# A decoder step on one core: conditioning rows out of prompt attention, its weights formed by two engines

## The chip, the cores and the metric

The kernel runs on one core of a Trainium2 chip. The metric is the device time in microseconds of one execution; 0.2% of it is 6.3 us.

## The reference

Two groups go through the same two layers: a prompt of 256 tokens and 8 samples of 8 new tokens with a cache of 256 tokens each, 320 rows of 2048 floats together. Everything is fp32. Cut to what matters:

```python
def ada_modulate(c, w, b):                      # 4 times: mixer and MLP of both layers
    m = jax.nn.silu(c) @ w + b                  # w: 2048 x 6144, c: 9 rows (1 prompt, 8 samples)
    shift, scale, gate = jnp.split(m[:, None, :], 3, axis=-1)
def diff_weights(s, lam):
    p = jax.nn.softmax(s, axis=-1)
    return p[:, :, 0] - lam * p[:, :, 1]
for layer in range(2):
    h = modulated_norm(x, norm_mix, shift, scale)
    y = even_mixer(h) if layer == 0 else odd_mixer(h)   # even: 8-head attention and RG-LRU
    x = x + gate * y
    shift, scale, gate = ada_modulate(c, ada_mlp_w[layer], ada_mlp_b[layer])
    h = modulated_norm(x, norm_mlp, shift, scale)
    x = x + gate * (jnp.square(jax.nn.relu(h @ w1)) @ w2)   # w1: 2048 x 8192
```

## The kernel before

Activations lie transposed, 16 tiles of 128 features by 320 tokens. Each weight matrix streams through four slots `raw` in chunks of 512 x 256 (512 KB). ScalarE copies a chunk to `w_hi` (L604), VectorE forms `w_lo` (L982), and TensorE makes three products per tile (hi.hi, hi.lo, lo.hi) to keep fp32 accuracy. `pair` on TensorE consumes four chunks into one pair of output tiles, 24 matmuls a chunk.

The conditioning vectors come from matrices of 2048 x 6144, read once each: 16 tiles of 128 rows by 2048 columns (1.05 MB) make one part, and (a, part) names it: a = 0 to 3 for mixer and MLP of layer 0, mixer and MLP of layer 1; part = 0, 1, 2 for shift, scale, gate. `part_tile` (TensorE, L1724) multiplies one tile with the 32 columns of `cs` in four strips, adding into a PSUM bank. Once 16 tiles are in, `ada_part` (VectorE, L1041) turns the bank and adds the bias. Where the tiles are fed:

- the input projection (layer 0): (0, *) and (1,0), with rows in `narrow`;
- query and key norms: (1,1), one tile a turn through `ada_wide` (TensorE L1732, SyncE L389), six slots;
- prompt attention: (1,2), two tiles in each `p_values` (L1967);
- sample attention: (2,0), two tiles a sample;
- the MLP of layer 0: `mlp_with_parts` (TensorE L2088) with `turn_with_part` (L1767; SyncE L415, called by `feed_with_ada` L489). A block has 16 pairs of chunks for w1 and 16 for w2. Blocks 0 to 3 take (2,1), (3,0), (3,1), (3,2) through the bank `acc` during w1, a tile ahead of every second chunk, and four tiles of (2,2) each through `acc_gate` in the first four pairs of w2. `narrow` then holds one tile: SyncE waits for `narrow_used` before it loads the next one, and the raw loads are behind that wait.

Work of each engine is written out in program order, and semaphores join the engines. Around the change this order is:

- Prompt attention, VectorE: for h = 0 to 8, `p_scores(h)` (scale, mask, two maxima; L1473), then `p_weights(h-1)` (reciprocals, factor lam, first product by TENSOR_SCALAR, second by SCALAR_TENSOR_TENSOR; L1484). ScalarE: four exponentials of head h with their sums (L842), the copy of the turned weights of head h-1 (L850) and of its output (L852). TensorE: scores of h+2, then in `p_values(h)` a tile, the turn of the weights, a tile, the value product.
- Sample attention: key pages of 8 samples are loaded by GpSimd's queue (`keys`, `values`, L554 and L562), each pair as soon as the pages two samples earlier are used; a sample's queue order is keys(b+1), values(b). TensorE: scores of b, turn of keys b+1, a tile, turn of weights, a tile, values of b.
- SyncE's `ada_wide` issues tile n once tile n-6 is used.

Of the kernel before, what the change touches and what calls it, by code (L numbers as in the profile page):

```python
# [9 lines left out]
ALU = mybir.AluOpType  # L10
# [3 lines left out]
P = 128  # L14
D = 2048
# [123 lines left out]
def trunk_kernel(nc, A, O):  # L139
    with ExitStack() as ctx:  # L140
# [113 lines left out]
        acc_gate = mm[:, 2, 1, :]  # L254
# [63 lines left out]
        p_score, p_max, p_exp, p_w, p_wT, p_pt, p_o, p_out = sems("p_score p_max p_exp p_w p_wT p_pt p_o p_out")  # L318
# [39 lines left out]
        MOD_READY = [8, 15, 21, 21]  # L358
# [7 lines left out]
        def _(sp):  # L366
# [102 lines left out]
            ada_wide(1, 2)  # L469
# [19 lines left out]
            def feed_with_ada(b, a, part, after):  # L489
# [7 lines left out]
                with looped(sp, 3, KT // 2, {K: 4}) as j:  # L497
                    load_quad(inward(W2, b, j))
# [5 lines left out]
            feed_with_ada(0, 2, 1, D)  # L504
            with looped(sp, 1, BLOCKS - 1, {K: 64, KN: 20}) as b:
                feed_with_ada(b, 3, b - 1, (b + 1) * D)
            feed_with_ada(3, 3, 2, None)
# [84 lines left out]
        def _(act):  # L592
# [242 lines left out]
            for h in range(H + 1):  # L835

                if h < H:
# [66 lines left out]
            act.wait_ge(wide_used, KT * 3)  # L904
# [58 lines left out]
        def _(dve):  # L963
# [308 lines left out]
            def outward(n, squares=True, mid=None):  # L1272

                per = {K: 8, G: 2, X: 2, steps: 2}
                if squares:
                    step(v.memset(sq_sum[:, :, :], 0.0))
                    settle()
                    per |= {SQ: 2, steps: 4}
                if mid is not None:
                    split()  # L1280
                    residual(0, 0, n, squares=squares)
                    split()
                    residual(1, 2, n, squares=squares)
                    mid()
                with looped(dve, 0 if mid is None else 1, 3 if squares else 4, per) as i:
# [24 lines left out]
            def mlp(n, last, parts=False):  # L1310
# [10 lines left out]
                def block_(ahead, part=None, squares=False, gate=False):  # L1321
# [5 lines left out]
                    if part is not None:  # L1327
                        NU.up(16)
                        ada_part(*part, acc, narrow_used, NU.now)
                        NU.up(4)  # L1330
                    if ahead:
                        outward(n, squares, (lambda: ada_part(2, 2, acc_gate, narrow_used, NU.now)) if gate else None)
# [9 lines left out]

                per = {G: 8, R: 8, U: 8, X: 8, steps: 8}
                if parts:
                    NU.up(24)
                    block_(1, (2, 1))
                    with looped(dve, 1, BLOCKS - 1, {K: 64, AG: 1, AT: 1, NU: 20, **per}) as b:
                        block_(1, (3, b - 1))
                    block_(1, (3, 2), squares=True, gate=True)
# [134 lines left out]
            def p_weights(h):  # L1484
# [5 lines left out]
                for k in (5, 7):  # L1490
                    step(v.tensor_tensor(small[:, r, k:k + 1], small[:, r, k:k + 1], lam[:, 0:1], ALU.mult))
                settle()
                for qb in range(2):
# [695 lines left out]
```

## Time and profile before

| | us |
|---|---|
| median of 3 runs | 3152.55 (3146.82 to 3153.94) |
| the profiled execution | 3152.81 |
| its span in the profile | 3151.1 |
| TensorE busy (share of the span) | 3056.1 (97%) |
| VectorE busy | 1480.9 (47%) |
| ScalarE busy | 1084.4 (34%) |
| moved by DMA | 624.90 MB, mean 198 GB/s |

The times of rows are microseconds from the start of the span. PE is TensorE (PEld its weight loads), DVE VectorE, ACT ScalarE, POOL GpSimd, SP SyncE. A bracket at the end of a timeline line gives the idle time of the engine before it and what ended it. An fp32 matmul has more than one record here (x8 is one tile of four matmuls). PEclk is the granted clock of TensorE in parts of 2.4 GHz, DMA share the mean busy share of the 16 engines.

### The profile page before, as it was taken

What the parts mean: (1) busy time and instruction counts of PE and PEld (TensorE: products, weight loads), DVE (VectorE), ACT (ScalarE), POOL (GpSimd) and SP (SyncE); (2) the same over time, 40 slices, a digit from 0 to 9 for tenths busy, and PEclk for the clock granted to TensorE, in tenths of its full rate; (3) what the DMA queues carried; (4) which work ended last, traced back from release to release, by engine and by line L of the source; (5) the groups of instructions that cost most, each with busy time, mean ns of one, the idle gap of its engine ahead of it and who ended that gap; (6) DMA issues with size and microseconds to landing.
All of it is one profiled execution on the core that took longest, in us unless ns stands there. A gap on an engine that the chain in (4) does not pass through costs nothing.

```text
span 3151.1 us, 53269 instructions
## 1 busy us (share of the span) xinstructions
PE 3056.1 (97%) x21011; PEld 2809.6 (89%) x21011; DVE 1480.9 (47%) x2057; ACT 1084.4 (34%) x1309; POOL 29.6 (1%) x55
## 2 busy tenths in 40 slices
PE   8999997899999999999999899999999999999998
PEld 4888853598899899889889899999899999999998
DVE  3556555455344344344345554445544444444443
ACT  3334443334322332332333433333433332332332
POOL 0000001000000000000000000000000000000000
PEclk8999998999999999999999999999999999999999
DMA  9986789545765765765774344444344444444543
GB/s 317 338 284 225 259 346 417 206 155 194 256 199 196 258 218 182 253 235 160 261 253 147 121 149 150 142 153 150 124 148 151 143 152 147 142 152 141 152 149 107
DMA packets 451959, 624.90 MB, mean 198 GB/s; under 512 B 16960, under 2 KB 402753, under 8 KB 433028
## 3 DMA queue, kind: packets, MB, share of 16 engines
q1 hardware_dynamic: 443776, 595.65, 57.1%
q0 software_dynamic: 6112, 22.84, 1.9%
q10 hardware_dynamic: 1926, 4.24, 0.4%
q8 instruction: 119, 1.95, 0.3%
q14 instruction: 26, 0.21, 0.0%
HBM read 617.13 MB, written 5.54 MB: 198 GB/s over the span
## 4 chain that ended last, share of the span: by engine, by line
PE 92%; DMA 4%; DVE 2%; issue 1%; ACT 1%; SPq 0%; POOL 0%; POOLq 0%; DVEq 0%; ACTq 0%
PE mm L1672 86%; PE aux L1672 5%; PE mm L1825 1%; DMA wide_first<-in_ada_mix_w 1%; DMA narrow<-in_ada_mlp_w 1%; DMA kpage<-in_cache_k 1%; DVE tmp L1063 1%; DMA vpage<-in_cache_v 1%; DMA second_row<-in_ada_mlp_w 0%; DVE h_lo L1089 0%; PE aux L2043 0%; DVE tmp L1079 0%; DVE tmp L1082 0%; DVE w_lo L982 0%; PE aux L1825 0%
## 5 line engine op out<-in xcount | busy, mean ns | idle before, releaser
L982 DVE TENSOR_TENSOR w_lo<-raw,w_hi 128x1024 fp32r<-128x1024 f32 x752 | 919.6, 1225 | 1325.9 <-ACT w_hi L604 1324.3
L604 ACT ACTIVATE w_hi<-raw 128x1024 fp32r<-128x1024 f32 x752 | 794.8, 1058 | 1703.9 <-PE mm L1672 1703.9
L1672 PE MATMUL mm<-h_hi,w_hi 128*128 128x320 f32 x3712 | 1167.6, 315 | 32.3 <-DVE h_lo L1089 18.9
L1672 PE MATMUL mm<-h_hi,w_lo 128*128 128x320 f32 x3712 | 1152.8, 311 | 0.0
L1672 PE MATMUL mm<-h_lo,w_hi 128*128 128x320 f32 x3712 | 1152.6, 311 | 0.0
L1672 PEld LDWEIGHTS mm<-h_hi,w_hi 128*128 128x128 f32 x3712 | 701.9, 189 | 132.8 <-issue 104.6
L1672 PE MATMUL mm<-u_hi,w_hi 128*128 128x320 f32 x2304 | 713.7, 310 | 0.0
L1672 PE MATMUL mm<-u_hi,w_lo 128*128 128x320 f32 x2304 | 712.0, 309 | 0.0
L1672 PE MATMUL mm<-u_lo,w_hi 128*128 128x320 f32 x2304 | 711.9, 309 | 0.0
L1672 PEld LDWEIGHTS mm<-h_lo,w_hi 128*128 128x128 f32 x3712 | 702.6, 189 | 0.2 <-issue 0.2
L1672 PEld LDWEIGHTS mm<-h_hi,w_lo 128*128 128x128 f32 x3712 | 702.2, 189 | 0.0
L1672 PEld LDWEIGHTS mm<-u_hi,w_hi 128*128 128x128 f32 x2304 | 432.5, 188 | 13.4 <-issue 13.4
L1672 PEld LDWEIGHTS mm<-u_lo,w_hi 128*128 128x128 f32 x2304 | 432.5, 188 | 0.0
L1672 PEld LDWEIGHTS mm<-u_hi,w_lo 128*128 128x128 f32 x2304 | 432.5, 188 | 0.0
L1672 PE MATMUL aux<-narrow,cs 128*32 128x512 f32 x856 | 122.0, 609 | 2.2 <-DMA narrow<-in_ada_mlp_w 2.2
L1318 DVE TENSOR_TENSOR u_lo<-mtmp,u_hi 128x640 f32 x64 | 52.8, 826 | 67.0 <-ACT u_hi L746 67.0
L746 ACT ACTIVATE u_hi<-mtmp 128x640 f32 x64 | 47.3, 739 | 98.5 <-DVE mtmp L1315 98.5
L1253 DVE SCALAR_TENSOR_TENSOR xT<-mm,mod,xT 128x256 f32 (+1 forms) x160 | 69.4, 476 | 0.0
L1315 DVE TENSOR_TENSOR mtmp<-mtmp 128x640 f32<-128x640 f32 x64 | 52.5, 820 | 0.0
L1672 PE MATMUL aux<-wide_first,cs 128*32 128x512 f32 x232 | 45.1, 679 | 5.8 <-DMA wide_first<-in_ada_mix_w 4.9
L744 ACT ACTIVATE mtmp<-mm 128x640 f32<-128x640 f32 x64 | 43.9, 686 | 0.0
L707 ACT ACTIVATE tmp<-tmp,mod,amp 128x256 f32<-128x256 f32 x64 | 34.0, 590 | 23.0 <-DVE amp L1070 14.6
(280 smaller groups left out, 1071.5 us busy)
## 6 DMA issues: line engine op xcount, KB each, us to landing
raw<-in_mlp_w SPq DMA_DIRECT2D x512, 512.0 KB, 3.7
narrow<-in_ada_mlp_w SPq DMA_DIRECT2D x70, 1024.0 KB, 5.0
raw<-in_w_in_odd SPq DMA_DIRECT2D x96, 512.0 KB, 3.8
narrow<-in_ada_mix_w SPq DMA_DIRECT2D x42, 1024.0 KB, 5.1
raw<-in_w_in_even SPq DMA_DIRECT2D x80, 512.0 KB, 6.9
wide_first<-in_ada_mix_w SPq DMA_DIRECT2D x58, 512.0 KB, 9.0
wide_later<-in_ada_mlp_w SPq DMA_DIRECT2D x20, 1024.0 KB, 14.3
raw<-in_w_out_even SPq DMA_DIRECT2D x32, 512.0 KB, 3.5
```

What stands on the lines that cost most here:

```text
L604: fn(w_hi[:, slot], raw[:, slot], ACT.Copy).then_inc(hi_ready, 1)
L707: ins = fn(out, out, ACT.Identity, scale=amp[:, k, 0:1], bias=mod[:, n, k, 0:1])
L744: fn(mtmp[:, r], mm[:, r, :, 0:T], ACT.Relu).then_inc(relu_out, 1)
L746: fn(u_hi[:, bass.ds(j, 2), :], mtmp[:, r], ACT.Copy).then_inc(u_hi_ready, 1)
L982: v.tensor_tensor(w_lo[:, slot], raw[:, slot], w_hi[:, slot].bitcast(F32), ALU.subtract).then_inc(lo_ready, 1)
L1063: v.tensor_tensor(tmp4[:, first // 4 % 2, first % 4:first % 4 + count], xT[:, first:first + count, :], rstd[:, :].unsqueeze(1).broadcast_t ...
L1253: ins = v.scalar_tensor_tensor(x, mm[:, r, m, 0:SEQ], g, x, ALU.mult, ALU.add)
L1315: v.tensor_tensor(mtmp[:, r], mtmp[:, r], mtmp[:, r], ALU.mult).then_inc(u_val, 1)
L1318: v.tensor_tensor(u_lo[:, bass.ds(j, 2), :], mtmp[:, r], u_hi[:, bass.ds(j, 2), :].bitcast(F32), ALU.subtract).then_inc(u_ready, 1)
L1672: return nc.tensor.matmul(out, lhsT, rhs, start=first, stop=last)
L1825: return nc.tensor.transpose(out, in_, const[0:rows, 0:rows])
```

## The change

Prompt attention has no conditioning tiles any more. (2,0) follows (1,1) directly in the six slots and is used in sample attention as before. (1,2) moves into the first MLP block through `acc`, which moves (2,1) to block 1, (3,0) to block 2 and (3,1) to block 3; (3,2) gets a bank of its own, `acc_last`, four tiles in each block, in pairs 5 to 8 of w2 (the second call of `turn_with_part` on `u_hi`). The 80 tiles of this MLP become 96. VectorE turns (1,2) after w1 of block 0 and waits for it before the first residual; it turns (2,2) and (3,2) in the last block after four residuals instead of (2,2) after two. In prompt attention ScalarE makes the first product (a copy with a column scale), and VectorE's reciprocals of head h-1 stand ahead of the scores of head h. Where loops had a common body, block by block is now written out.

```diff
@@ SyncE
             ada_wide(1, 1, 2)
-            ada_wide(1, 2)
             ada_wide(2, 0)
...
                 turn_with_part(inward(W2, b, 1), 2, 2, b * (4 * P), inward(W2, b, 2))
-                with looped(sp, 3, KT // 2, {K: 4}) as j:
+                turn_with_part(inward(W2, b, 3), 3, 2, b * (4 * P), inward(W2, b, 4))
+                with looped(sp, 5, KT // 2, {K: 4}) as j:
                     load_quad(inward(W2, b, j))
...
-            feed_with_ada(0, 2, 1, D)
-            with looped(sp, 1, BLOCKS - 1, {K: 64, KN: 20}) as b:
-                feed_with_ada(b, 3, b - 1, (b + 1) * D)
-            feed_with_ada(3, 3, 2, None)
+            feed_with_ada(0, 1, 2, D)
+            feed_with_ada(1, 2, 1, 2 * D)
+            feed_with_ada(2, 3, 0, 3 * D)
+            feed_with_ada(3, 3, 1, None)
@@ ScalarE
             for h in range(H + 1):
+                if h >= 1:
+                    r = (h - 1) % 2
+                    act.wait_ge(p_part, h)
+                    for qb in range(2):
+                        part = p_s[:, r, 0, 0:P] if qb == 0 else p_s[:, r, 0, P:384]
+                        ins = fn(part, part, ACT.Copy, scale=small[:, r, 4 + 2 * qb:5 + 2 * qb])
+                    ins.then_inc(p_first, 1)
...
-            act.wait_ge(wide_used, KT * 3)
+            act.wait_ge(wide_used, KT * 2)
@@ VectorE
+                with looped(dve, 0, 2, per) as i:
+                    split()
+                    residual(0, i * 4, n, squares=squares)
+                    split()
+                    residual(1, i * 4 + 2, n, squares=squares)
                 if mid is not None:
-                    split()
-                    residual(0, 0, n, squares=squares)
-                    split()
-                    residual(1, 2, n, squares=squares)
                     mid()
-                with looped(dve, 0 if mid is None else 1, 3 if squares else 4, per) as i:
+                with looped(dve, 2, 3 if squares else 4, per) as i:
...
                         ada_part(*part, acc, narrow_used, NU.now)
-                        NU.up(4)
+                        NU.up(8)
+                        dve.wait_ge(mod_ready, AG.now)
...
+                def last_parts():
+                    ada_part(2, 2, acc_gate, narrow_used, NU.now - 4)
+                    ada_part(3, 2, acc_last, narrow_used, NU.now)
...
-            def p_weights(h):
+            def p_parts(h):
                 r = h % 2
                 dve.wait_ge(p_exp, h + 1)
                 step(v.reciprocal(small[:, r, 4:8], small[:, r, 4:8]))
                 settle()
-                for k in (5, 7):
-                    step(v.tensor_tensor(small[:, r, k:k + 1], small[:, r, k:k + 1], lam[:, 0:1], ALU.mult))
-                settle()
-                for qb in range(2):
-                    keys = slice(0, P) if qb == 0 else slice(P, 384)
-                    step(v.tensor_scalar(p_s[:, r, 0, keys], p_s[:, r, 0, keys], small[:, r, 4 + 2 * qb:5 + 2 * qb], None,
-                                         ALU.mult))
-                settle()
+                step(v.tensor_tensor(small[:, r, 5:6], small[:, r, 5:6], lam[:, 0:1], ALU.mult))
+                v.tensor_tensor(small[:, r, 7:8], small[:, r, 7:8], lam[:, 0:1], ALU.mult).then_inc(p_part, 1)
+
+            def p_weights(h):
+                r = h % 2
+                dve.wait_ge(p_part, h + 1)
+                settle()
+                dve.wait_ge(p_first, h + 1)
                 for qb in range(2):
...
             for h in range(H + 1):
+                if h >= 1:
+                    p_parts(h - 1)
                 if h < H:
                     p_scores(h)
...
-                if b == 0:
-                    ada_part(1, 2, acc, wide_used, 2 * KT)
@@ TensorE
             def p_values(h):
                 r = h % 2
-                ada_wide()
                 pe.wait_ge(p_w, h + 1)
...
                 ins.then_inc(p_wT, 1)
-                ada_wide()
                 pe.wait_ge(p_pt, h + 1)
...
                     turn_with_part(u_hi, u_lo, acc_gate, 4 * b, u_block(),
                                    ((relu_out, relu - 1), lambda: (relu_out, relu)))
-                    with looped(pe, 1, 4, {K: 8, G: 2}):
+                    turn_with_part(u_hi, u_lo, acc_last, 4 * b, None, (None, None))
+                    with looped(pe, 2, 4, {K: 8, G: 2}):
```

## Rows read from the trace of the kernel before

**Rows 1.** The page, part 4: shares of the chain that ended last.

```profile
...
PE 92%; DMA 4%; DVE 2%; issue 1%; ACT 1%; SPq 0%; POOL 0%; POOLq 0%; DVEq 0%; ACTq 0%
...
```

**Rows 2.** Windows: prompt attention, then sample attention (header: columns).

```profile
...
core 0: us, PE busy (x) PEld busy (x) DVE busy (x) ACT busy (x) POOL busy (x), PEclk, DMA share, GB/s
...
468.30:516.10 47.80, 39.51 (x264) 17.30 (x264) 29.85 (x83) 21.08 (x80) 3.23 (x6) 0.86 1.02 420
516.10:599.40 83.30, 68.18 (x944) 39.86 (x944) 34.12 (x116) 12.97 (x24) 13.67 (x26) 0.92 0.85 345
...
```

**Rows 3.** Chain of waits, 400 to 630: start us, us, what held it.

```profile
...
497.94 15.76 DMA narrow<-in_ada_mlp_w
...
524.46 21.18 DMA kpage<-in_cache_k
...
```

**Rows 4.** Timeline of DVE, sample attention: three of eight score evacuations (start us, us).

```profile
...
521.38 0.42 DVE L1536 TENSOR_SCALAR s_s<-mm 128x256 f32<-128x256 f32 x1 [1.50 <-PE mm L1672]
...
584.89 0.42 DVE L1536 TENSOR_SCALAR s_s<-mm 128x256 f32<-128x256 f32 x1 [7.35 <-PE mm L1672]
...
593.03 0.42 DVE L1536 TENSOR_SCALAR s_s<-mm 128x256 f32<-128x256 f32 x1 [3.27 <-PE mm L1672]
...
```

**Rows 5.** Timeline of PE in sample attention: two stalls on page transfers.

```profile
...
539.06 0.64 PE L2043 MATMUL aux<-vpage,s_pt 128*32 128x128 f32 x16 [2.21 <-DMA vpage<-in_cache_v]
...
545.68 3.68 PE L1825 MATMUL mm<-const,kpage 128*128 128x128 f32 x16 [2.40 <-DMA kpage<-in_cache_k]
...
```

**Rows 6.** Chain of waits, an MLP block of layer 0.

```profile
...
1118.06 0.99 PE aux L1672 x8
1119.06 124.62 PE mm L1672 x848
...
```

**Rows 7.** Chain of waits, layer 1: one whole MLP block.

```profile
...
2449.23 225.68 PE mm L1672 x1536
...
```

**Rows 8.** Groups of instructions in the MLP block of rows 6.

```profile
...
L982 DVE TENSOR_TENSOR w_lo<-raw,w_hi 128x1024 fp32r<-128x1024 f32 x64 | 78.4, 1226 | 139.0 <-ACT w_hi L604 139.0
...
```

**Rows 9.** Timeline of DVE in prompt attention.

```profile
...
491.25 0.96 DVE L1478 SCALAR_TENSOR_TENSOR p_s<-mm,const 128x768 f32<-128x768 f32 x1 [0.71 <-PE mm L1825]
...
493.17 0.17 DVE L1488 RECIPROCAL small<-small 128x4 f32<-128x4 f32 x1
...
493.64 0.55 DVE L1495 TENSOR_SCALAR p_s<-p_s,small 128x128 f32<-128x128 f32 x2
494.23 0.75 DVE L1500 SCALAR_TENSOR_TENSOR p_s<-p_s,small 128x128 f32<-128x128 f32 x2
495.69 0.96 DVE L1478 SCALAR_TENSOR_TENSOR p_s<-mm,const 128x768 f32<-128x768 f32 x1 [0.72 <-PE mm L1825]
...
509.24 0.18 DVE L1488 RECIPROCAL small<-small 128x4 f32<-128x4 f32 x1 [3.28 <-ACT p_s L842]
...
```

**Rows 10.** Timeline of ACT in prompt attention.

```profile
...
507.07 0.38 ACT L852 ACTIVATE pj<-aux 128x256 f32<-128x256 f32 x1 [4.43 <-PE aux L1672]
507.36 0.39 ACT L842 ACTIVATE p_s<-p_s,small 128x128 f32<-128x128 f32 x1
...
507.74 0.39 ACT L842 ACTIVATE p_s<-p_s,small 128x128 f32<-128x128 f32 x1
...
509.11 0.47 ACT L850 ACTIVATE p_t<-mm 128x384 f32<-128x384 f32 x1
...
```

**Rows 11.** Timeline of PE in prompt attention.

```profile
...
475.94 0.90 PE L1825 MATMUL mm<-const,p_s 128*128 128x128 f32 x3 [1.08 <-DVE p_s L1500]
...
483.19 0.94 PE L1672 MATMUL aux<-p_t,vtok 128*128 128x128 f32 x6
...
505.57 1.47 PE L1672 MATMUL aux<-p_t,vtok 128*128 128x128 f32 x6
...
```

**Rows 12.** One line, L707: ns min/median/max of one, over the span.

```profile
...
L707 ACT ACTIVATE tmp<-tmp,mod,amp x64: 583/587/603, 51.5 to 2227.8; 128x256 f32<-128x256 f32 x64
...
```

**Rows 13.** Window at the start of prompt attention, columns of rows 2.

```profile
...
470.00:475.00 5.00, 4.14 (x19) 1.13 (x16) 4.83 (x13) 2.66 (x13) 1.13 (x2) 0.50 1.01 421
...
```

More of the change, by code:

```diff
@@ L253, in trunk_kernel @@
         acc = aux[:, 1, :]
-        acc_gate = mm[:, 2, 1, :]
+        acc_gate, acc_last = mm[:, 2, 1, :], mm[:, 2, 0, :]
         folded = mm[:, 2, 1, 448:448 + 4 * NC]
@@ L317, in trunk_kernel @@
         tok_t, tok_ready = sems("tok_t tok_ready")
-        p_score, p_max, p_exp, p_w, p_wT, p_pt, p_o, p_out = sems("p_score p_max p_exp p_w p_wT p_pt p_o p_out")
+        p_score, p_max, p_exp, p_part, p_first, p_w, p_wT, p_pt, p_o, p_out = sems(
+            "p_score p_max p_exp p_part p_first p_w p_wT p_pt p_o p_out")
         tab_in = sems("tab_in")
@@ L357, in trunk_kernel @@
         GAIN = [ROW["norm_mix"], ROW["norm_mlp"], ROW["norm_mix"] + KT, ROW["norm_mlp"] + KT]
-        MOD_READY = [8, 15, 21, 21]
+        MOD_READY = [8, 14, 21, 21]
         H_READY = [0, 10, 16, 22]
@@ L1329, in block_ @@
                         ada_part(*part, acc, narrow_used, NU.now)
-                        NU.up(4)
+                        NU.up(8)
+                        dve.wait_ge(mod_ready, AG.now)
                     if ahead:
-                        outward(n, squares, (lambda: ada_part(2, 2, acc_gate, narrow_used, NU.now)) if gate else None)
+                        outward(n, squares, last_parts if gate else None)
                     else:
@@ L1345, in mlp @@
                     NU.up(24)
+                    block_(1, (1, 2))
                     block_(1, (2, 1))
-                    with looped(dve, 1, BLOCKS - 1, {K: 64, AG: 1, AT: 1, NU: 20, **per}) as b:
-                        block_(1, (3, b - 1))
-                    block_(1, (3, 2), squares=True, gate=True)
+                    block_(1, (3, 0))
+                    block_(1, (3, 1), squares=True, gate=True)
                 else:
@@ L1559, in _ @@
                               ).then_inc(s_pte, 1)
-            ada_part(2, 0, acc, wide_used, 3 * KT)
+            ada_part(2, 0, acc, wide_used, 2 * KT)
             dve.wait_ge(s_root, 1)
@@ L2090, in mlp_with_parts @@
                 for b in range(BLOCKS):
-                    pe.wait_ge(ada_turned, b + 4)
+                    pe.wait_ge(ada_turned, b + 3)
                     turn_with_part(h_hi, h_lo, acc, 0, h_inputs(count),
```

## The prediction

> **What bounds the kernel now.** I read the page first. Its chain of waits is TensorE for 92% of the span and DMA for 4% [rows 1], so nearly everywhere a microsecond of TensorE work is a microsecond of time, and DMA decides only in some stretch. The question is which. Windows by stage answer it: in prompt attention (468.3 to 516.1, 47.8 us) the DMA share is 1.02 at 420 GB/s, TensorE is busy 39.51 us of 47.80; in sample attention (516.1 to 599.4, 83.3 us) DMA runs at 345 GB/s on average and TensorE is busy 68.18 us [rows 2]. The chain inside this stretch, read next, goes through transfers: the last conditioning rows for 15.76 us, then a key page for 21.18 us [rows 3]. So these two stages are partly DMA-bound, and everything behind them is TensorE-bound. The change takes 16 transfers of 1.05 MB (128 rows of 2048 floats) out of the DMA-bound part and puts them, with the TensorE work that belongs to them, where TensorE is the bound. It trades one against the other, and the sum is that of both.
>
> **Sample attention.** First I look for the undisturbed pace. The eighth score evacuation comes 593.03 - 584.89 = 8.14 us after the seventh, with no DMA wait between; the first comes 521.38 - 516.1 = 5.3 us after the stage begins, and the stage ends 599.4 - 593.03 = 6.4 us after the eighth [rows 2, 4]. Undisturbed the stage is 5.3 + 7 x 8.14 + 6.4 = 68.7 us. It takes 83.3, so waits for transfers (and the slower TensorE beside them) hold 14.6 us. That is the upper bound of the gain here.
>
> How much of it goes? The stage still consumes per sample two conditioning tiles, one pair of key pages and one pair of value pages, four units of 1.05 MB in 8.14 us: 515 GB/s, against 420 served [rows 2]. It can only run at the undisturbed pace from stock and by a growing backlog. Stock: in the new order the six tile slots are refilled with rows of (2,0) as the query/key stage uses up (1,1), and nobody uses them in prompt attention, so six tiles, two key pairs and one value pair lie ready; today the queue is full when the stage begins. Left to come are 10 tiles, 6 key pairs and 7 value pairs: 23 units, 24.1 MB, 57 us at 420 GB/s, which just fits into 62 us. But the shares of the two queues decide. A value wait ended at 539.06 and the key wait behind it on GpSimd's queue at 545.68: with SyncE's queue also full, one unit of pages takes 6.6 us [rows 5], that is 0.159 of 0.420 MB/us, 38%. From 2.6 us after the start until the tiles begin (8.2 us) the pages have the engines alone, 2.5 us a unit: 2.2 units. SyncE then gets 0.26 MB/us, 4.0 us a tile, so its 10 tiles keep it busy until about 48 us; in these 40 us the pages get 6.0 units, 8.2 in all. At the undisturbed pace PE wants its ninth page unit at about 46 us. So some 0.8 units (5 us at this share) are missing there once, with landing on top; afterwards the pages have the engines alone and catch up. I take 5 us of stall left, gain 9.6. Bounds: 14.6, and 4 (the stage begins with five tiles less queued, 12 us of transfers, of which at least a third should show).
>
> The Trainium skill, DMA: Bandwidth & Descriptors, "Queues, rings and completion order", says that each DMA engine takes turns between the queues that have work, a packet each. Equal packets would give the pages half of the bandwidth, a unit in 5 us instead of the 6.6 of rows 5, and the missing 0.8 units would be there in time; the trace speaks against an even share. What the sum would be by an even share is the third rival.
>
> **The MLP.** Sixteen tiles are added in front of pairs of weight chunks: four per block on (3,2) in the second down pair, while the others keep their number. What does one cost? A stretch of 17 chunk pairs and 4 tiles takes 124.62 us [rows 6]. A block of layer 1 without tiles takes 225.68 us for 1536 matmuls, 32 chunk pairs of 48: 7.05 us each [rows 7]. So 4 tiles take 124.62 - 17 x 7.05 = 4.7 us, 1.18 us each; the 0.99 of the chain's own row for the tile [rows 6] misses the slowed first weights behind it. The cost is 16 x 1.18 = 18.8 us. All of it is on the path. Bounds: 15.8 (0.99 each) and 18.9.
>
> What else comes with it, at nothing: the 16 transfers (2.5 us each at 420 GB/s) go to `narrow`, one slot, and SyncE waits on it with the raw loads behind; it did so for 80 tiles already, in blocks where TensorE never waited, and VectorE sits idle 139 us of a 249 us block before its weight halves [rows 8], which is the cover. If it failed, each raw load that came late would cost its lateness. The turning of (1,2) and (3,2) (about 1 us of VectorE each) lies in the same cover, as does the new wait for `mod_ready` in front of the first residual, behind which stand a split and the residual; both have a chunk pair of 7 us. Loops written out or re-entered cost VectorE and SyncE sequencer time only.
>
> **Prompt attention.** Its undisturbed period today is 495.69 - 491.25 = 4.44 us a head [rows 9], in which the two tiles on TensorE and the chain scores, reductions, weights, turn just fit. The change takes the tiles away (2 us of TensorE), and the first factor from VectorE (494.23 - 493.64 = 0.59 us [rows 9]). But it also puts the reciprocal of head h-1 in front of the scores of head h, and that waits for ScalarE's exponentials. The new circle: exponentials 509.24 - 507.36 = 1.88 us from their start to the reciprocal [rows 9, 10]; reciprocal and factors 0.47; scores and maxima 493.17 - 491.25 = 1.92 [rows 9]; a handover of 0.03. That is 4.30 us. The other circle, through ScalarE: exponentials to the copy of the turned weights 509.11 - 507.36 = 1.75, that copy 0.47, PE's value product 0.94 [rows 11] with 0.10 of handovers, the output copy 0.29 to the next start, and the two new scaled copies [rows 10]. For these I have no row. Nearest are the exponentials with one column operand on the same tiles, 0.39 and, by the stretch from 507.36 to 509.11, about 0.49, less the overlap of 0.1 each: 0.69. The upper bound is twice L707, 128x256 with two column operands: 1.17 [rows 12]; the lower two plain copies, 0.5. I take 0.69, since shape and operands are nearest: 4.24 us, just under 4.30. By the Trainium skill, ScalarE: Activation LUTs, "What ACT_TABLE_LOAD costs", each column pointer adds about 93 ns; a copy with one pointer would then cost what the exponential does without its read-out, again 0.69, while L707 has two.
>
> So VectorE's relief is eaten by the new order: the period falls only from 4.44 to 4.30, and the gain is the DMA waits. In full: first scores 1 us after 468.3, maxima 1.92 later (471.2), exponentials to 473.1, factors and second scores to 475.5; six periods to 501.3 for the eighth maxima; then exponentials, value product and output of the head before, its own copies (4.24), products 0.75, turn some 0.6 (0.90 at the low clock [rows 11]), copy, value product, output copy with handovers 2.0: 7.6, so 508.9 against 516.1. Gain 7.2 with TensorE at full clock.
>
> Its clock is the doubt. With two tiles of 0.99 us [rows 6] gone, TensorE pauses 2 us more in every head. After the pauses at the beginning of this stage the granted clock was 0.50, the lower level of 1.2 GHz [rows 13]; there the turn took 0.90 and a value product 1.47 (full clock: 0.94) [rows 11]. ScalarE's circle then is 4.24 + 0.53 = 4.77. With half of the heads like that it costs 3.5 x 0.47 = 1.6, and 0.6 more in tail and at the start of the sample stage. Gain 7.2 - 2.2 = 5.0. Bounds: 7.2, and 7.2 - 7 x 0.95 = 0.5 with the low clock throughout and copies at their upper bound (period 5.25).
>
> **Sum.** 18.8 - 9.6 - 5.0 = +4.2 us. The profiled execution took 3152.8 us (span 3151.1 and 1.7 around it), the median of three runs 3152.55, so both are one level: 3157.0 us. A measurement of this kernel tells 0.2% (6.3 us) from nothing; the forecast is no measurable change, leaning to slower.
>
> **The rivals.**
> 1. Slower: the pages stay late. GpSimd's queue keeps its 6.6 us a unit and falls behind earlier than I count, so that 11 of the 14.6 us of stall stay. For it: demand is over supply all the time, and a stall also lowers TensorE's clock (the 3.68 us turn behind a wait [rows 5]). Against it: the stock at the start. Price: 18.8 - 3.6 - 4 = +11, 3164. It decides slower once more than 7 us of stall stay with the prompt gain at 5.
> 2. Slower: TensorE stays at the low clock through prompt attention and into the first samples. The prompt stage gains 1, the sample stage 8: +10, 3163. For it: rows 13. Against: the clock of prompt attention averages 0.86 [rows 2], so it came back within the stage, beside DMA waits that now go.
> 3. No change from the other side: full clock and no stall: 18.8 - 7.2 - 14.6 = -3, 3150. With an even share of the queues (a page unit in 2 x 2.5 = 5 us beside SyncE's, 8 instead of 6 in the 40 us, nothing missing at 46 us) it comes out near here: 1 us of stall and prompt gain 5, so 18.8 - 13.6 - 5 = +0.2, 3153. The even share is the rule of the skill's page named above.
> 4. Faster: rival 3's gains in full, and the moved tiles hide a part of their 1.18 us under the matmuls around them (0.75 each, 7 us less): 3143. For it: a tile uses 32 columns of TensorE. Against: [rows 6] show no such overlap.
> 5. The cover fails: SyncE's waits delay raw loads. One chunk late by 2 us per block, +8: 3165. Nothing in 80 tiles shows it.
>
> **How the numbers follow.** Chances: forecast 0.48, rival 1 0.20, rival 2 0.10, rival 3 0.13, rival 4 0.06, rival 5 0.03. Slower by over 0.2%: rivals 1, 2 and 5, less a little near the line, plus the upper edge of the forecast: 0.33. Faster: 0.07. Within: 0.60. The range runs from rival 3 to rival 1: 3149 to 3165.
>
> **What would show it.** Blocks of layer 0's MLP longer by 4.7 us each (249.0 to 253.7) show the cost; any other growth says that tiles or waits are priced wrong. Prompt attention of 40 to 47 us with DMA mostly idle in its second half; a period of 4.3, or 4.8 where the granted clock is 0.5. In sample attention a period of 8.14 for the first five or six samples, and a page wait of about 5 us once near the end; stalls from the third sample on would show rival 1. The forecast is wrong if the two stages together gain under 12 us or over 25.

## The result and the profile after

The changed kernel takes 3163.29 us (median of 9 runs, 3158.06 to 3168.18), the kernel before 3149.89 (9 runs beside it, 3146.31 to 3153.94): ratio 1.0041, 95% interval 1.0032 to 1.0050. It is slower by 13.4 us, by more than the 0.2% that a measurement tells. The forecast was 3157.0, +4.2, inside "no measurable change". The profiled executions stand only 8.1 us apart (3160.94 and 3152.81, spans 3159.3 and 3151.1); of the 5.3 us between that and the medians, 2.9 are the profiled execution before, which lay above its median, and 2.4 the changed one, which lay below.

The page of the changed kernel, shares of the chain that ended last; it answers to [rows 1]:

```profile
PE 93%; DMA 2%; DVE 2%; ACT 1%; issue 1%; SPq 0%; POOL 0%; POOLq 0%; DVEq 0%; ACTq 0%
```

DMA went from 4% to 2%: half of the time on transfers left the path. Windows of the changed kernel for prompt and sample attention (columns of [rows 2]), then its first five microseconds of scores, which answer to [rows 13]:

```profile
467.56:511.79 44.23, 25.15 (x137) 17.20 (x137) 25.47 (x67) 26.50 (x96) 3.23 (x6) 0.72 0.44 176
511.79:591.79 80.00, 67.06 (x949) 40.47 (x950) 34.49 (x116) 16.39 (x37) 13.68 (x26) 0.95 0.76 303
...
469.00:474.00 5.00, 1.18 (x11) 0.53 (x8) 3.90 (x10) 2.66 (x10) 1.14 (x2) 0.97 1.00 419
```

Prompt attention was bound by DMA (share 1.02); now DMA stands at 0.44, and TensorE's mean granted clock fell from 0.86 to 0.72. The first scores ran at full clock this time (0.97 against 0.50); the low clock came later, with 0.50 between 475 and 480. The stage gained 47.85 - 44.23 = 3.6 us. Sample attention, by DVE's score evacuations ([rows 4]), third to fifth and last of eight:

```profile
534.55 0.42 DVE L1554 TENSOR_SCALAR s_s<-mm 128x256 f32<-128x256 f32 x1 [3.27 <-PE mm L1688]
543.86 0.42 DVE L1554 TENSOR_SCALAR s_s<-mm 128x256 f32<-128x256 f32 x1 [4.45 <-PE mm L1688]
557.23 0.42 DVE L1554 TENSOR_SCALAR s_s<-mm 128x256 f32<-128x256 f32 x1 [3.42 <-PE mm L1688]
...
581.63 0.42 DVE L1554 TENSOR_SCALAR s_s<-mm 128x256 f32<-128x256 f32 x1 [3.27 <-PE mm L1688]
```

The eighth comes 581.63 - 511.79 = 69.84 us after the stage begins; before it was 76.89 (593.03 - 516.14). Two intervals are longer than 8.14: 9.31 and 13.37, 6.4 us more. They are page waits, with a slower turn of the keys behind the second (2.73 for 1.97). PE's timeline, answering to [rows 5]:

```profile
540.65 0.64 PE L2057 MATMUL aux<-vpage,s_pt 128*32 128x128 f32 x16 [1.43 <-DMA vpage<-in_cache_v]
...
547.79 2.73 PE L1841 MATMUL mm<-const,kpage 128*128 128x128 f32 x16 [4.00 <-DMA kpage<-in_cache_k]
```

In the chain (start, us, what) the first row below lies under both waits; the second ends in a wait of only 0.23 us. These two answer to [rows 3], the third, an MLP half of layer 0 with w2, to [rows 6]:

```profile
529.49 18.26 DMA kpage<-in_cache_k
...
560.30 13.32 DMA kpage<-in_cache_k
...
1113.47 129.37 PE mm L1688 x880
```

The half took 124.62 for x848 before: 4.75 us more, 32 matmuls more being the four tiles. In DVE's groups the cover of [rows 8] is intact (141.5 us idle ahead of `w_lo` in a block).

Prompt attention of one head at full clock, ACT's timeline (start us, us, ...), answering to [rows 10]; new are the scaled copies, L843:

```profile
495.24 0.47 ACT L859 ACTIVATE p_t<-mm 128x384 f32<-128x384 f32 x1
496.74 0.38 ACT L861 ACTIVATE pj<-aux 128x256 f32<-128x256 f32 x1 [1.02 <-PE aux L1688]
497.02 0.79 ACT L843 ACTIVATE p_s<-p_s,small 128x128 f32<-128x128 f32 x2
...
499.53 0.47 ACT L859 ACTIVATE p_t<-mm 128x384 f32<-128x384 f32 x1
```

and PE's for the end of one such head and for the next, which fell to the low clock ([rows 11]):

```profile
500.05 0.94 PE L1688 MATMUL aux<-p_t,vtok 128*128 128x128 f32 x6 [0.76 <-ACT p_t L859]
503.02 0.90 PE L1841 MATMUL mm<-const,p_s 128*128 128x128 f32 x3 [2.04 <-DVE p_s L1516]
504.50 1.65 PE L1688 MATMUL aux<-p_t,vtok 128*128 128x128 f32 x6 [0.58 <-ACT p_t L859]
```

The period is 499.53 - 495.24 = 4.29, as forecast. At the low clock a value product takes 1.65, and the head 5.09.

Stage by stage, from the profiles (us). A profile is one execution, a median is that of 6 to 12, and each ratio is to the kernel before as it ran beside that experiment, with medians of 3149.89 to 3151.24. ("prompt" runs from the first scores to the first turn of keys, "samples" from there to the eighth evacuation, "MLP 0" from its norm's squares to those of the next; "last MLP" is layer 1's, from its norm's squares to the turning of the output, which the change does not touch.)

| kernel | prompt | samples | MLP 0 | last MLP | median | ratio to before, 95% |
|---|---|---|---|---|---|---|
| before | 47.85 | 76.89 | 1007.66 | 924.77 | 3149.89 | |
| changed | 44.23 | 69.84 | 1026.67 | 924.06 | 3163.29 | 1.0041, 1.0032 to 1.0050 |
| split_only | 47.83 | 78.43 | 1007.71 | 923.30 | 3149.62 | 0.9999, 0.9990 to 1.0008 |
| move_only | 42.67 | 70.69 | 1026.63 | 924.72 | 3157.82 | 1.0021, 1.0012 to 1.0030 |
| no_last_part | 47.91 | 71.35 | 1007.64 | 924.58 | 3142.56 | 0.9973, 0.9963 to 0.9984 |
| idle_tiles | 43.64 | 68.36 | 1026.64 | 923.82 | 3159.97 | 1.0030, 1.0021 to 1.0040 |
| copies_first | 41.06 | 73.99 | 1026.64 | 923.66 | 3158.37 | 1.0025, 1.0015 to 1.0034 |
| early_page | 44.24 | 69.87 | 1026.67 | 924.50 | 3161.30 | 1.0036, 1.0024 to 1.0048 |
| sample_from_memory | 47.90 | 63.13 | 1026.63 | 926.19 | 3156.93 | 1.0016, 1.0007 to 1.0025 |
| half_moved | 42.74 | 75.79 | 1024.53 | 921.33 | 3155.91 | 1.0020, 1.0011 to 1.0029 |
| before_early_page | 50.36 | 72.15 | 1007.64 | 921.62 | 3149.89 | 0.9999, 0.9990 to 1.0007 |
| gap_tiles | 47.76 | 80.04 | 1006.16 | 925.17 | 3149.38 | 0.9998, 0.9989 to 1.0007 |
| copies_idle | 42.29 | 68.25 | 1027.39 | 915.10 | 3149.80 | 1.0005, 0.9995 to 1.0014 |
| short_tiles | 47.89 | 70.92 | 1026.66 | 915.11 | 3152.99 | 1.0008, 0.9997 to 1.0020 |

### The profile page after: what moved, and what is told of

Its sections match the earlier page's. It is cut to its first block, busy times and chain, and to the rows that moved or that the text cites. A ratio compares the mean times of both kernels' runs of the same rounds, so it can differ in the third digit from the quotient of the medians.

```text
span 3159.3 us, 52905 instructions
## 1 busy us (share of the span) xinstructions
PE 3056.7 (97%) x21011; PEld 2811.7 (89%) x21011; DVE 1476.3 (47%) x2041; ACT 1089.8 (34%) x1325; POOL 29.6 (1%) x55
## 3 DMA queue, kind: packets, MB, share of 16 engines
q10 hardware_dynamic: 1926, 4.24, 0.4%
## 4 chain that ended last, share of the span: by engine, by line
PE 93%; DMA 2%; DVE 2%; ACT 1%; issue 1%; SPq 0%; POOL 0%; POOLq 0%; DVEq 0%; ACTq 0%
PE mm L1688 87%; PE aux L1688 5%; PE mm L1841 1%; DMA kpage<-in_cache_k 1%; DMA wide_first<-in_ada_mix_w 1%; DMA second_row<-in_ada_mlp_w 0%; DVE tmp L1072 0%; ACT p_s L851 0%; DVE h_lo L1098 0%; PE aux L2057 0%; DVE tmp L1088 0%; DVE tmp L1091 0%; ACT p_s L843 0%; DVE w_lo L991 0%; ACT p_t L859 0%
## 5 line engine op out<-in xcount | busy, mean ns | idle before, releaser
L708 ACT ACTIVATE tmp<-tmp,mod,amp 128x256 f32<-128x256 f32 x64 | 34.0, 590 | 23.0 <-DVE amp L1079 14.6
```

What stands on the lines that cost most here:

```text
L708: ins = fn(out, out, ACT.Identity, scale=amp[:, k, 0:1], bias=mod[:, n, k, 0:1])
```

## The experiments

**The two halves of the change.** split_only is the kernel before with the weights formed by two engines and the tiles left in prompt attention; move_only is the changed kernel with VectorE alone forming the weights (its old `p_weights` and order).

```
 # move_only, against the changed kernel: ScalarE
-                if h >= 1:
-                    act.wait_ge(p_part, h)
-                    ...  (the two scaled copies)
 # and VectorE: p_weights(h - 1) behind p_scores(h), as before
```

> The kernel before with one part of the change: ScalarE makes the first product, reciprocals ahead of the scores; the 16 tiles stay in prompt attention. Mine: the stage is bound by transfers and the circle falls only from 4.44 to 4.30 us a head, so prompt attention stays at 47 to 48 us and the time at that of before, within 2 us. Rival (VectorE is the bound of a head, so 0.6 us less a head counts): 3 to 5 us faster.

> The changed kernel with VectorE forming the weights as before; all tiles moved. Mine: circle scores, weights, turn of the weights 4.4 us a head at full clock and about 4.8 at the low one, so prompt attention takes 43 to 46 us, and the time is that of the changed kernel within 3 us (above before by 8 to 14 us). Rival (the split pays once the tiles are gone): slower than the changed kernel by 4 us or more.

The split alone is worth nothing (0.9999): prompt attention stays DMA-bound at 47.83. But on top of the moved tiles it costs: without it the changed kernel is 5.5 us faster in the medians, although its circle at full clock is longer (4.43 against 4.29). The expectation (within 3 us) missed, and that contradicts the step that took the split for a small gain.

**The cost of the tiles in the MLP.** no_last_part leaves out the transfers and multiplications of the 16 tiles of (3,2); VectorE still turns a bank in their place, that of (2,2).

```
-                    turn_with_part(u_hi, u_lo, acc_last, 4 * b, None, (None, None))
-                    with looped(pe, 2, 4, {K: 8, G: 2}):
+                    with looped(pe, 1, 4, {K: 8, G: 2}):
 # SyncE
-                turn_with_part(inward(W2, b, 3), 3, 2, b * (4 * P), inward(W2, b, 4))
+                load_quad(inward(W2, b, 3))
+                load_quad(inward(W2, b, 4))
```

> The changed kernel without the 16 tiles of (3,2): neither loaded nor multiplied (its values are left out of the result). Mine: every block's second half takes 124.6 us instead of 129.4, and the time falls by 19 us against the changed kernel, to some 6 to 11 us below before: what the attention stages alone gain. Rival (waits on the one narrow slot or on instruction loading are part of the cost): falls by more than 22 us.

MLP 0 falls back to 1007.64, 19.03 us less: 1.19 per tile, all on the path. The medians say 20.7. Yet with the tiles gone for nothing the kernel is only 7.3 us faster than before, so the attention stages give back some 7, not 14.6. And its prompt attention, the same code as the changed kernel's, took 47.91, no gain at all. The window of this kernel's prompt attention, then PE's and ACT's timelines for one head:

```profile
463.66:511.57 47.91, 30.96 (x137) 21.31 (x137) 25.48 (x67) 26.70 (x96) 3.23 (x6) 0.56 0.41 163
```
```profile
492.46 0.90 PE L1842 MATMUL mm<-const,p_s 128*128 128x128 f32 x3 [0.45 <-DVE p_s L1517]
493.95 1.65 PE L1689 MATMUL aux<-p_t,vtok 128*128 128x128 f32 x6 [0.58 <-ACT p_t L860]
495.52 1.66 PE L1689 MATMUL mm<-pj 64*128 64x128 f32 x8
```
```profile
493.40 0.49 ACT L860 ACTIVATE p_t<-mm 128x384 f32<-128x384 f32 x1
495.63 0.38 ACT L862 ACTIVATE pj<-aux 128x256 f32<-128x256 f32 x1 [1.74 <-PE aux L1689]
495.91 0.79 ACT L844 ACTIVATE p_s<-p_s,small 128x128 f32<-128x128 f32 x2
496.60 0.39 ACT L852 ACTIVATE p_s<-p_s,small 128x128 f32<-128x128 f32 x1
...
498.57 0.49 ACT L860 ACTIVATE p_t<-mm 128x384 f32<-128x384 f32 x1
```

This is ScalarE's circle: copies 495.91 to 496.60 (0.69, as taken), exponentials until the copy of the turned weights 1.97, that copy and the handover 0.54, TensorE's value product 1.65 and 0.04, output copy 0.28 to the next start: 5.17. ScalarE sits idle 1.74 us behind the value product in every head. The granted clock is 0.56 on average, near the lower level of 1.2 GHz.

**Is it the clock?** idle_tiles puts back two multiplications of a tile's shape per head, from constants, without transfers.

```
+            def idle_tile():
+                cols = const[:, 0:D].rearrange("p (t s i) -> p s t i", s=4, i=32)
+                for n in range(4):
+                    mul(acc[32 * n:32 * n + 32, :].rearrange("p (t i) -> p t i", i=32), cs[:, 0, :], cols[:, n], True, True)
 # in p_values, ahead of the turn and ahead of the value product
+                idle_tile()
```

> The changed kernel with two tiles' worth of matmuls per head in prompt attention from a constant already in memory, no transfer, result thrown away. Mine (TensorE's clock falls in the pauses that the tiles left): granted clock near 1.0 in the stage, every head 4.3 to 4.5 us instead of 4.3 and 5.1 by turns, prompt attention 40 to 42 us instead of 44.2, the first key turn 2.0 us instead of 3.4: 3 to 6 us faster than the changed kernel, and with less spread between runs. Rival (the clock costs nothing here, the circle is ScalarE's and VectorE's): no faster, or slower by the added matmuls.

The clock rises to 0.88 in that window, as it was before the change, but the prompt stage falls to 43.64 only, not to the 40 to 42 expected. The tiles seem to stand in the circles too: heads take 4.44 to 4.46, and the third, still at the low clock, 5.71. By the medians it is worth 3.3 us, with intervals that overlap. Work for its own sake gets the clock, not the circle.

**Is it the order on ScalarE?** copies_first breaks the circle: the output copy of head h-2 goes behind the scaled copies of h-1, so that no copy of ScalarE's waits for the product just issued.

```
                 ... the two scaled copies of h - 1
+                if h >= 2:
+                    act.wait_ge(p_o, h - 1)
+                    fn(pj[:, h - 2, 0:SEQ], p_sum((h - 2) % 2), ACT.Copy).then_inc(p_out, 1)
                 ... exponentials of h, copy of the turned weights of h - 1
-                    act.wait_ge(p_o, h)
-                    fn(pj[:, h - 1, 0:SEQ], p_sum((h - 1) % 2), ACT.Copy).then_inc(p_out, 1)
                 ... the output copy of the last head behind the loop
```

> The changed kernel with ScalarE's order in prompt attention altered: the output copy of head h-2 stands behind the scaled copies of head h-1, no longer ahead of them, so ScalarE does not wait for a value product before it can begin the next exponentials. Mine (the split made a circle exponentials, copy, value product at the low clock, output copy, scaled copies of 5.1 to 5.2 us): every head after the second 4.3 us whatever the clock, prompt attention 40.5 to 42.5 us, time 4 to 7 us below the changed kernel, at or just below the kernel with the tiles moved and VectorE alone (3157.8). Rival (the scaled copies themselves or the wait for the exponentials cost it): within 1.5 us of the changed kernel.

The prompt stage takes 41.06 us with the granted clock at 0.68: six of seven periods are 4.28 or 4.29 (one is 4.61), where the changed kernel's order gives 5.17 at the low clock. The medians gain 4.9 us. It is the order that makes the low clock cost: with the other one the circle stayed VectorE's in all heads but one. But the sample stage then starts at the low clock (first evacuation after 8.0 us instead of 5.24 at full clock) and takes 73.99: of the 6.8 us against 47.9, 3 are lost again behind (70.92 in short_tiles below, whose prompt stage took 47.89).

**Does one page make the sample stall?** early_page loads the second value page in the prompt stage, before_early_page does that to the kernel before.

```
-            for b in range(NB):
-                if b + 1 < NB:
-                    keys(b + 1)
-                values(b)
+            keys(1)
+            values(0)
+            values(1)
+            ...  (b from 1: keys(b + 1), and values(b) from b = 2)
```

> The changed kernel with the value pages of sample 1 loaded during prompt attention, ahead of GpSimd's wait for the first key turn. Mine (the sample stage runs from stock against a queue that gives pages 6.6 us a unit): one page unit more in stock, so of some 7 us of stall 3 to 6 go; sample evacuations from first to eighth fall from 63 to about 59 us, time 3 to 6 below the changed kernel. Rival (the stall is total bandwidth or SyncE's tiles): no change in the stall, time within 1.5 us of the changed kernel.

> The kernel before with the value pages of sample 1 loaded during prompt attention. Mine: transfers are the bound of both stages and their sum is unchanged, so the order moves only the tail: 0 to 2 us faster, in all likelihood not to be told from before. Rival (the pages' place in the queue is what the sample stage waits for): 4 us faster or more.

No, against the expectation of 3 to 6 us: 69.87 against 69.84, the sum of the intervals from the first sample to the eighth 63.2 in both. Only the places of the waits moved. On the kernel before the same edit changes nothing either (0.9999); its profile shows 2.5 us lost in prompt and 4.7 won in samples.

**Is it all transfers of the stage together?** sample_from_memory takes the operands of the 16 (2,0) tiles of sample attention from memory that is there already; the transfers are left out.

```
+                cols = xT[:, :, :].rearrange("p k t -> p (k t)")[:, 0:D].rearrange("p (t s i) -> p s t i", s=4, i=32)
```

> The changed kernel with the 16 tiles of (2,0) in sample attention multiplied from activations already in memory: the same TensorE work, no transfer (the values of (2,0) are left out of the result). Mine (the stall left in sample attention is the sum of all transfers requested after the stage begins, 24 MB at 420 GB/s): with 13.6 MB left the evacuations follow every 8.1 us, 57 us from first to eighth instead of 63 to 64, and the time is 6 to 8 us below the changed kernel. Rival (GpSimd's queue gives 6.6 us a unit whatever SyncE's does): stalls of 5 us or more remain.

DVE's first, second and eighth score evacuations in this kernel:

```profile
520.04 0.42 DVE L1553 TENSOR_SCALAR s_s<-mm 128x256 f32<-128x256 f32 x1 [1.50 <-PE mm L1687]
528.03 0.42 DVE L1553 TENSOR_SCALAR s_s<-mm 128x256 f32<-128x256 f32 x1 [3.27 <-PE mm L1687]
...
576.84 0.42 DVE L1553 TENSOR_SCALAR s_s<-mm 128x256 f32<-128x256 f32 x1 [3.27 <-PE mm L1687]
```

(576.84 - 520.04) / 7 = 8.11: the undisturbed pace. The first-to-eighth stretch is 56.8 us here and 63.2 in the changed kernel: the 6.4 us of page waits come from the tile transfers beside the pages, all of them. The medians differ by 6.4 us, which is the same size but no proof: the profiles also differ by 3.7 in prompt and by 2.1 in the last MLP, both against this kernel.

**Half the move.** half_moved is the kernel before with VectorE's weights and only 8 tiles moved, one tile a head left in prompt attention (the 8 tiles of (2,0)'s second half are loaded in the first MLP block).

```
-            ada_wide(2, 0)
+            ada_wide(2, 0, 0, KT // 2)
 # p_values: the second ada_wide() goes
 # first MLP block, ahead of the third pair with a tile
+                        if b == 0 and i == 2:
+                            pe.wait_ge(ada_turned, 4)
```

> The kernel before (VectorE forms the weights) with 8 tiles moved instead of 16: one tile a head in prompt attention, two a sample, the last eight of (2,0) in the first MLP block. Mine: MLP plus 8 x 1.18 = 9.4 us; prompt attention 41 to 44 us (a tile a head keeps TensorE busier and the transfers fit), sample attention 74 to 77 us as in the changed kernel, since its stock is the same: 131 us become 117 to 120, so 2 to 5 us below before. Rival (the eight tiles left keep the queue full, the stall stays that of before): 0 to 8 us above before.

A miss by my own edit: MLP 0 grew by 16.9 instead of 9.4. PE's timeline holds one gap of 5.7 us up to 807.39, TensorE waiting for VectorE's turning, and the chain 1.7 us of slower multiplications behind it. Without these 7.4 it would stand at 3149 by estimate, no better than before: the attention stages gave 6.2 us (5.1 and 1.1), the tiles cost the other 9.5, and 3.4 came from the last MLP, which the edit does not touch.

**A free place for tiles?** gap_tiles (from before) puts four tiles of (2,1) into TensorE's pause at the norm ahead of the first MLP.

```
+                if gap:
+                    sp.dma_start(second_row, ada_rows(ADA[a], P, part)).then_inc(wide_in[0], 16)
+                    ...  (tiles 0, 2 and 3 through narrow, one after the other)
```

> The kernel before, with four tiles of (2,1) multiplied in the pause of TensorE during the norm ahead of the first MLP (one before the norm's sums, three after, the second from a slot of its own) instead of between chunk pairs; one of the four stood in the pause already. Mine (a tile costs 1.18 us between chunk pairs and nothing in a pause): the first block is shorter by 3.5 us, the norm's end no later: 3 to 4.5 us below before. Rival (the tiles delay the norm's sums or the first weights, or TensorE's clock): no gain, or up to 3 us above before.

```profile
742.99 1.06 PE L1681 MATMUL aux<-narrow,cs 128*32 128x512 f32 x8 [1.41 <-DMA narrow<-in_ada_mix_w]
749.17 1.93 PE L1681 MATMUL aux<-narrow,cs 128*32 128x512 f32 x8 [5.11 <-DMA narrow<-in_ada_mix_w]
```

PE's timeline shows why: through one slot each tile takes some 5 us to come, and TensorE waits 5.11 for the last. 1.5 of the 3.5 us expected remain in MLP 0, nothing in the medians.

**Both repairs together.** copies_idle is copies_first with one idle tile per head.

> The changed kernel with ScalarE's output copy behind the scaled copies, and one tile's worth of matmuls from a constant per head, result thrown away. Mine (after the order of ScalarE is mended, what is left of the low clock is the slow start of sample attention, 8.0 us to the first evacuation instead of 5.2, and a slow last value product): granted clock of prompt attention 0.85 or more, first evacuation at 5.3 to 6, time 1 to 4 us below the kernel with that order alone (3158.4), 6 to 9 below the changed kernel. Rival (TensorE's clock is of no account once nobody waits for its products): within 1 us of 3158.4.

The median is 3149.80, level with before and 8.6 below copies_first (6.3 by the ratios), where 1 to 4 were expected. The table says where the profiles differ: 5.7 won in samples, 1.2 lost in prompt, 0.75 in the MLP, and 8.56 won in the last MLP, which none of it touches. That is 12.3 us together, more than the medians give; how much of the gain in samples a usual execution has is not shown. Chains of the last MLP, the changed kernel's first:

```profile
2237.58 218.47 PE mm L1688 x1488
2456.05 1.49 issue
2457.54 2.43 PE mm L1688 x15
2459.97 1.05 issue
2461.02 223.24 PE mm L1688 x1521
2684.26 2.02 issue
...
2912.03 1.77 issue
2913.80 227.07 PE mm L1688 x1536
```
```profile
2231.85 894.33 PE mm L1689 x6096
```

The changed kernel (as the one before, 2.01, 1.85 and 1.87 in front of blocks like that of [rows 7]) pauses at each turn of the block loop with no wait that the profile shows; copies_idle does not. Its instruction queue fetched less. The page's line of that queue (packets, MB, share), changed kernel, then copies_idle:

```profile
q8 instruction: 125, 2.05, 0.3%
```
```profile
q8 instruction: 98, 1.61, 0.2%
```

**Is that where the code lies?** short_tiles is the changed kernel with as many added matmuls as copies_idle, of 32 columns, in one place beside a wait.

```
+                if h == 0:
+                    pe.wait_ge(ada_turned, 2)
+                    for _ in range(8):
+                        idle_tile()
 # in idle_tile
+                    mul(acc[32 * n:32 * n + 32, 0:32], cs[:, 0, :], cols[:, n, 0], True, True)
```

> The changed kernel with 32 idle multiplications of 32 columns (8 idle tiles of 4, cut from 512 columns) put all in one place, where TensorE waits for the first head's weights. They add as many instructions to TensorE's program ahead of the last MLP as the idle tiles of copies_idle did, but almost no work (under 2 us, beside a wait) and nothing to the head circles. Theory A (where the last MLP's code lies decides its 'issue' gaps): last MLP 894.3 us instead of 903.3, no gap of over 0.5 us in its chain, 98 packets on the instruction queue instead of 125, the median 9 below the changed kernel's, 3154 +-2; the prompt stage stays at 44 to 48. Theory B (the gaps went in copies_idle because of the higher clock or the copy's place ahead of it): last MLP 902 to 904, 125 packets, the median 3163 +-2. In both the prompt attention is a second look at the changed kernel's: 44.2 if the profiled execution was typical, 47.9 (circles of 5.17 at the low clock, as no_last_part and sample_from_memory showed) if it was a lucky one; the mean of the two by the medians.

Yes, in so far as instructions that do almost no work removed the pauses. This is its last MLP, then its prompt attention:

```profile
2239.20 894.33 PE mm L1688 x6096
```
```profile
462.89:510.78 47.89, 31.65 (x200) 21.95 (x200) 25.48 (x67) 26.69 (x96) 3.23 (x6) 0.56 0.41 164
```

98 packets, 894.33 to the hundredth (the table's stage 915.1, 9.0 less than the changed kernel's), and a median 10.3 below the changed kernel's. 32 short matmuls on TensorE make an unrelated stage 9 us shorter. What exactly of the position decides (which boundary the loop crosses) stays open; idle_tiles, with twice as many, has the gaps. The second reading bears on the changed kernel's 2.4 us between profile and median: the same attention code, the last four heads at 5.16 to 5.17, gives 47.89. Of four profiles of this order beside other edits (early_page, no_last_part, sample_from_memory, short_tiles) three show no gain; and the two that show the gain were fast executions of their kernels, the changed kernel's the second fastest of nine and early_page's the fastest of six. So the gain of 3.6 us is probably not what a usual execution has. The profiles part at the third head. In both kernels of the timelines above it runs at the low clock behind a pause of TensorE of 4.0 us; one head later the changed kernel's turn takes 0.55 again (at 480.85), that of no_last_part still 0.90 (at 476.96), and so it stays. Why is open.

By stages the change is then 0 in prompt attention, -6.0 (70.92) to -7.0 in samples, +19.0 in the MLP: +12 to +13, against 13.4 measured. The opening, up to the first prompt scores, varies from 462.7 to 468.3 us between the profiles whatever the edit, so single profiles are compared here by stages and not by their spans, and two or three microseconds of any one comparison stay unexplained.

## Where the prediction was right, and which step failed

It said +4.2 where +13.4 was measured. The range (3149 to 3165) held the time, in part by luck: its upper end was set by late pages (rival 1), and what came was nearer to rival 2. The base was off as well, since 3152.8 is 2.9 above the median of nine.

**The cost in the MLP: right.** 18.8 forecast, 19.0 measured (1026.67 - 1007.66), 4.75 per half; the cover of the transfers held, so rival 5 fell.

**The prompt term: the step that failed.** The forecast had 5.0; the profiled execution gave 3.6, and three of the five profiles of this order give 0. Its pieces: the VectorE circle 4.30 (measured 4.29) and the scaled copies 0.69 (0.69) were right. The low clock was mis-sized in two ways. First the circle: "ScalarE's circle then is 4.24 + 0.53 = 4.77". It is 5.17. The 1.47 us of [rows 11] is not the low clock's full price; there the product takes 1.65 (+0.18). And the turn, 0.90 at that clock, ends after the exponentials, so the copy of the turned weights waits for it: 1.97 instead of 1.75 (+0.22). Second the share: "with half of the heads like that". In three of four other profiles of this order the last four heads all are, and the third is half (4.93). Against the 40.6 us of the full-clock working, short_tiles' 47.89 has 4.1 more in its seven periods (34.2 against 30.1) and 3.2 more in the tail behind the eighth scores, where turn, product and copy follow each other at that clock; the changed kernel's profile has 1.4 and 2.3 more.

That comes close to rival 2 ("TensorE stays at the low clock through prompt attention and into the first samples", prompt gain 1, sample gain 8, 3163). It had a chance of 0.10. What spoke for it was in [rows 13], 0.50 beside pauses; what spoke against it, 0.86 over the stage, was a mean taken with the two tiles in each head, which are what the change removes. idle_tiles shows that: with such tiles back, 0.88.

**The sample term: right in kind, off by 2.6.** 9.6 forecast, 7.05 in the profile. The stall left was said to be 5 us, once, near the end; it was 6.2 (the two long intervals, less a short first one), between the third and the fifth sample's scores: PE waited for a value page at 540.65, 29 us after the start instead of about 46, and the key page behind it let PE go on 7.1 us later, where [rows 5] had 6.6. The rest, 1.4, is the slow start at the low clock (6.64 against 5.24). Of the 14.6 us 7.6 stayed, where rival 1 (the pages stay late) had 11. Rival 3's even share did not come: a page unit took 7.1 us beside SyncE's transfers, again far from the 5 of an even share. The Trainium skill, DMA: Bandwidth & Descriptors, "Queues, rings and completion order", has the engines alternate packet by packet between queues. The step from there to half of the bandwidth does not hold in the trace: between 540.65 and 547.79 GpSimd's queue moved 295 packets with 1.08 MB and SyncE's 257 with 1.93 MB, and between 539.06 and 545.68 of the kernel before it was 248 with 0.89 MB and 246 with 1.88 MB. These packets of the profile came nearly one for one, which fits the alternation, but the pages' hold half as many bytes, so the pages got 36% and 32% of the traffic. Whether the profile counts the same packets as the rule no run here shows.

**Full-clock profit of the split: wrong in sign.** The forecast gave it a period of 4.30 for 4.44. But it also tied ScalarE's circle to TensorE's clock: move_only, whose ScalarE has slack, has heads of 4.43 to 4.79 at a granted clock of 0.66 and is 5.5 us faster. And at full clock it buys nothing even by the forecast's own timeline: the reciprocals stand ahead of the second head's scores too, so that the first period is 4.29, where the old order has 2.89 (before and move_only). Seven periods are 30.0 us in the new order and 2.89 + 6 x 4.44 = 29.5 in the old one.

**Not foreseen: the last MLP.** Before and changed kernel both hold its gaps (924.77, 924.06), so it did not move this comparison; it moved those of experiments by up to 11 us between kernels (915.1 to 926.2).

No version beat the kernel before: copies_idle and short_tiles reach its time only through the 9 us of the last MLP, which it might win as well by added instructions of its own. That was not run.

## What to carry to other kernels

Moving work out of a transfer-bound stage into a compute-bound one pays its full price at once (here 1.19 us a tile), while the gain in the stage left is capped by the next circle: write that circle down with every TensorE product on it at the low clock, since the work taken away is what kept the clock up. When an instruction is put in front of another engine's wait, check that no producer-consumer circle through the slowest clock closes in one iteration; delaying an output copy by one iteration opened it here for 5 us. And read two kernels by stage: a stage that neither edit touches can differ by 10 us.

## What the hardware showed that I had not expected

A loop of 1536 matmuls per turn on TensorE paused at its turns, 1.35 to 2.2 us and in some kernels up to 1.15 us more a little later, or never, according to what stood ahead of it in the program (32 matmuls more removed the pauses, 64 did not): 98 packets (1.61 MB) on the instruction queue without the pauses, 118 to 126 (1.93 to 2.06 MB) with them, for the same work. The stage is 6 to 11 us longer with them.
